# Prologue projections as three float32r products, with a narrower weight ring and subtractions on GpSimd

## What is computed

```python
def token_mixer(h, w_in, b_in, ...):
    p = h @ w_in + b_in
    y_a = hyena_branch(p[..., :ML_START], ...)
    y_b, state = mlstm_branch(p[..., ML_START:GATE_START], p[..., GATE_START:MERGE_START], ..., state0)
    g_a, g_b = jnp.split(jax.nn.sigmoid(p[..., MERGE_START:]), N_BRANCHES, axis=-1)
    y = (g_a * (y_a @ w_branch_hy) + g_b * (y_b @ w_branch_ml)) @ w_out
    return y, state

# first block, x and ctx both (1, 256, 1024)
ada_x = jnp.split(s_lat @ w_ada[l] + b_ada[l], 6, axis=-1)          # modulation, likewise ada_c
pc = hc @ w_in[l][:, ML_START:MERGE_START] + b_in[l][ML_START:MERGE_START]
_, ctx_state = mlstm_branch(pc[..., :ML_COLS], pc[..., ML_COLS:], ..., mlstm_zero_state(B))
yx, _ = token_mixer(hx, *mix_params, rows, GRID_W, ctx_state)
x = x + ada_x[2][:, None, :] * yx
x = x + ada_x[5][:, None, :] * expert_choice_ffn(hx2, w_router[l], w_exp1[l], w_exp3[l], w_exp2[l])
```

## Time and profile before

| | us |
|---|---|
| median of three runs | 2400.16 |
| lowest, highest | 2399.78, 2400.80 |
| profiled execution, its own time | 2399.33 |
| its span | 2397.5 |
| TensorE products busy | 2026.2 (85%) |
| VectorE busy | 823.2 (34%) |
| ScalarE busy | 596.3 (25%) |
| GpSimd busy | 0.2 (4 instructions) |
| DMA | 660.82 MB, 276 GB/s on average |
| mean granted TensorE clock | 0.916 of 2.4 GHz |

### The profile page before, as it was taken

The page is one execution under the profiler, slowest core; times in us unless marked ns, Lnnn a source line. Parts: engine busy times, 40 slices in busy tenths (PEclk is TensorE's granted clock), DMA queues, the critical chain, the costliest instruction groups (busy, mean ns, idle before and its releaser), DMA issues.

```text
span 2397.5 us, 28400 instructions
## 1 busy us (share of the span) xinstructions
PE 2026.2 (85%) x12394; PEld 1414.0 (59%) x12394; DVE 823.2 (34%) x1053; ACT 596.3 (25%) x698; POOL 0.2 (0%) x4
## 2 busy tenths in 40 slices
PE   7999997666666667666666899999999999989998
PEld 3586673222222222222222799888999999888998
DVE  4423523000000000000001655566555555557554
ACT  3311201000000000000001433563434433554333
POOL 0000000000000000000000000000000000000000
PEclk9999998888888877778888899999999999999999
DMA  9137255999999999999999445434544545434542
GB/s 395 71 145 329 88 236 216 436 429 432 433 430 432 433 429 434 431 429 434 431 429 430 156 180 197 185 124 152 199 176 176 224 176 195 186 120 150 197 181 97
DMA packets 34092, 660.82 MB, mean 276 GB/s; under 512 B 3784, under 2 KB 4296, under 8 KB 6224
## 3 DMA queue, kind: packets, MB, share of 16 engines
q1 hardware_dynamic: 31984, 651.60, 66.0%
q10 hardware_dynamic: 2016, 7.84, 0.9%
HBM read 658.38 MB, written 1.05 MB: 275 GB/s over the span
## 4 chain that ended last, share of the span: by engine, by line
PE 63%; DMA 29%; DVE 5%; ACT 2%; issue 1%; SPq 0%; ACTq 0%; DVEq 0%
PE ps L1329 62%; DMA ring_b<-experts_dram 19%; DMA ring<-experts_dram 9%; PE ps L1338 1%; DVE ring_lo L1104 1%; ACT w_hi L579 1%; DVE mixer_area L1254 0%; DVE att_area L1250 0%; ACT att_area L700 0%; ACT expert_area L558 0%; DVE tail L942 0%; DVE u_lo L1145 0%; DVE tail L949 0%; ACT u_hi L610 0%; DVE area_h L1084 0%
## 5 line engine op out<-in xcount | busy, mean ns | idle before, releaser
L1104 DVE TENSOR_TENSOR ring_lo<-ring,w_hi 128x2048 fp32r<-128x2048 f32 x168 | 384.9, 2292 | 242.0 <-ACT w_hi L579 242.0
L1329 PE MATMUL ps<-u_hi,w_hi 128*128 128x256 f32 x1536 | 435.5, 284 | 0.0
L1329 PE MATMUL ps<-u_hi,ring_lo 128*128 128x256 f32 x1536 | 432.8, 282 | 0.0
L1329 PE MATMUL ps<-u_lo,w_hi 128*128 128x256 f32 x1536 | 432.0, 281 | 0.0
L579 ACT CAST w_hi<-ring 128x2048 fp32r<-128x2048 f32 x168 | 320.0, 1905 | 201.5 <-PE ps L1329 200.4
L1329 PEld LDWEIGHTS ps<-u_lo,w_hi 128*128 128x128 f32 x1536 | 291.5, 190 | 1.8
L1329 PEld LDWEIGHTS ps<-u_hi,w_hi 128*128 128x128 f32 x1536 | 289.7, 189 | 2.5 <-issue 0.7
L1329 PEld LDWEIGHTS ps<-u_hi,ring_lo 128*128 128x128 f32 x1536 | 289.5, 188 | 0.0
L1329 PE MATMUL ps<-ring,area_h 128*32 128x512 f32 (+1 forms) x1088 | 185.3, 768 | 70.4 <-DMA ring<-experts_dram 62.6
L1329 PE MATMUL ps<-ring_b,area_h 128*32 128x512 f32 x1024 | 160.9, 792 | 81.0 <-DMA ring_b<-experts_dram 72.6
L558 ACT COPY expert_area<-ps 128x1024 f32<-128x1024 f32 x16 | 16.2, 1012 | 616.3 <-PE ps L1329 616.3
(11 more groups left out here) (311 smaller groups left out, 2126.6 us busy)
## 6 DMA issues: line engine op xcount, KB each, us to landing
ring<-stream_dram SPq DMA_DIRECT2D x116, 2048.0 KB, 8.0
ring_b<-experts_dram SPq DMA_DIRECT2D x48, 4096.0 KB, 31.0
ring<-experts_dram SPq DMA_DIRECT2D x48, 4096.0 KB, 31.0
area_n<-norm_rows_dram ACTq DMA_DIRECT2D x6, 512.0 KB, 4.5
tail<-filt_out_dram SPq DMA_DIRECT2D x1, 1536.0 KB, 6.5
tables<-tabs_dram ACTq DMA_DIRECT2D x1, 1408.0 KB, 13.2
tabs<-tabs_dram ACTq DMA_DIRECT2D x1, 1296.0 KB, 10.4
x_tok<-x_dram SPq DMA_DIRECT2D x1, 1024.0 KB, 9.7
```

The source lines that it names most:

```text
L1104: V.tensor_tensor(ring_lo[:, n % RING, :], ring[:, n % RING, :], upper_part(n).bitcast(F32), ALU.subtract).then_inc(sig("alone_ready") if ...
L1329: ins = M.matmul(out, lhsT, rhs, start=start, stop=stop, **more)
```

## The change

All projections of the prologue (gates, k, q, v, o, Hyena, merge, branches, output) become three float32r products. The modulation products and the short ones (filters, spectra, states, heads, transforms, router) stay float32.

The parts:

- **Inputs.** The normed, modulated input is kept as upper and lower float32r parts, `xT` for x and `cT` for the context, apart from each other. ScalarE writes the upper parts from PSUM, VectorE writes exact copies (`exact`) and subtracts. The gates' weights, the branch inputs (`y_r`) and the merged sums (`merge_r`) are split too; the merged sum of one k takes four VectorE operations instead of two.
- **Weights.** 30 of the slots are split. ScalarE casts each (`upper_first`) into one of three upper buffers: `x_r`, which lies over `x_tok`, and the former ring places 6 and 7; from the 25th on `area_hr` takes the place of `x_r`. The lower part is written over the slot, for 12 slots by VectorE (`lower_first`), for 18 (`BY_POOL`) by GpSimd, which had no work before. x is loaded a second time, since `x_r` overwrites it.
- **Ring.** After the first eight slots the ring has six places (three pairs), not eight. There are 54 slots, not 56.
- **Order.** Gates and k are computed together in passes over k; the context follows the x part. v comes ahead of q. In the loop over q and Hyena each turn is two units and two modulation slots (rows 1 and 2 both), so that the heads have no modulation. o is computed between the context states. All 16 merge units come after those. The merge units 25 to 31 are kept without the sigmoid, which then runs once over all seven. The branches are done in half passes of four k, mLSTM branch first.
- **Waits.** The second half of the first expert's blocks waits for all 54 slots.

```diff
+FIRST_RING = 6
+ADA_SLOTS = (tuple(range(8)), (13, 14, 16, 17, 19, 20, 22, 23), (25, 26, 28, 29, 31, 32, 34, 35))
+FIRST_SPLIT = (8, 9, 10, 11, 12, 15, 18, 21, 24, 27, 30, 33) + tuple(range(36, FIRST_SLOTS))
+BY_POOL = (0, 1) + tuple(range(12, 28))
+HEAD_UNITS = ((25, 26), (27,), (28, 29), (30,))
...
+            for i in range((FIRST_SLOTS - RING) // 2):
+
+                sp.wait_ge(sig("slot_used"), 2 * i + (2 if i < 3 else 4))
+                if 2 * i + 4 == FIRST_SPLIT[21] + 1:
+                    sp.dma_start(x_tok[:, :, :], d["x"]).then_inc(sig("x_loaded"), 16)
+                load(i % 3, PAIRS + i)
...
+            def upper_first(i):
+
+                n = FIRST_SPLIT[i]
+                act.wait_ge(sig(f"pair_loaded{first_place(n) // 2}"), first_turn(n) * 16 + 16)
+                if i == 0:
+                    act.wait_ge(sig("norm_ready"), TT)
+                elif i < 3:
+                    act.wait_ge(sig("slot_used"), RING)
+                else:
+                    act.wait_ge(sig("slot_used"), FIRST_SPLIT[i - 3] + 1)
+                A.copy(first_upper(i), ring[:, first_place(n), :]).then_inc(sig("first_hi"), 1)
...
+            for i in range(8):
+                upper_first(6 + i)
+                for c in (4 + 2 * i, 5 + 2 * i):
+                    to_conv(c, col("b_q", c - 4) if c < 8 else col("b_hy", c - 8), T)
...
+            def lower_first(i):
+
+                dve.wait_ge(sig("first_hi"), i + 1)
+                at = first_place(FIRST_SPLIT[i])
+                V.tensor_tensor(ring_lo[:, at, :], ring[:, at, :], first_upper(i).bitcast(F32),
+                                ALU.subtract).then_inc(sig("first_lo"), 1)
...
+                total = expert_area[:, 2048 + k % 2 * T:2048 + (k % 2 + 1) * T]
                 step(V.tensor_tensor(m, bank(k % 4), m, ALU.mult))
-                V.tensor_tensor(merge[:, k, 0, :], merge[:, k, 0, :], merge[:, k, 1, :],
-                                ALU.add).then_inc(sig("merged"), 1)
+                step(V.tensor_tensor(total, merge[:, k, 0, :], merge[:, k, 1, :], ALU.add))
+                step(V.tensor_copy(merge_r[:, k, 0, :], total))
+                V.tensor_tensor(merge_r[:, k, 1, :], total, merge_r[:, k, 0, :].bitcast(F32),
+                                ALU.subtract).then_inc(sig("merged"), 1)
...
+        @block.gpsimd
+        def _(pool):
+            for i in BY_POOL:
+
+                pool.wait_ge(sig("first_hi"), i + 1)
+                at = first_place(FIRST_SPLIT[i])
+                nc.gpsimd.tensor_tensor(ring_lo[:, at, :], ring[:, at, :], first_upper(i).bitcast(F32),
+                                        ALU.subtract).then_inc(sig("first_lo_p"), 1)
...
+            def unit(b, i, j):
+
+                w = split_first(i)
+                for k in range(KD):
+                    a = j * 1024 + k * P
+                    last = k == KD - 1
+                    product3(b[:, 0:T], [v[:, a:a + P] for v in w], [v[:, k, :] for v in xT], k == 0, last,
+                             free=int(last and j == 1), ready=sig("unit_ready") if last else None)
...
+            for i in range(8):
+                for j in range(2):
+                    unit(unit_bank(5 + 2 * i + j), 4 + i, j)
+                if i % 4 == 0:
+                    pe.wait_ge(sig("v_kept"), 1 if i == 0 else 2 * TT)
+                ada(4 if i < 4 else 7, range(2 * (i % 4), 2 * (i % 4) + 2), 1 + i // 4)
+                if i == 5:
+                    ada_turn(1, 4)
```

More of the change, by code:

```diff
@@ new lines, in _ @@
+            for k in range(KD):
+                pe.wait_ge(sig("hT_hi"), 1 + k + 1)
+                for u in range(4):
+                    for p in range(2 if u < 3 else 1):
+                        mm(bank(u)[:, 0:T], first_four(u, p, k), xT[0][:, k, :], start=k == p == 0, stop=False)
+                if 1 <= k <= 4:
+                    pe.wait_ge(sig("hT_tmp"), k)
+                    turned_in(k + 3)
+            pe.wait_ge(sig("first_lo_p"), 2)
+            for k in range(KD):
+                pe.wait_ge(sig("hT_lo"), 1 + k + 1)
+                for u in range(4):
+                    mm(bank(u)[:, 0:T], first_four(u, 0, k), xT[1][:, k, :], start=False,
+                       stop=u < 3 and k == KD - 1)
+                    if u == 3:
+                        mm(bank(u)[:, 0:T], first_four(u, 1, k), xT[0][:, k, :], start=False, stop=k == KD - 1)
@@ new lines, in with_context @@
+            def with_context(u, b):
+                for k in range(KD):
+                    if u == 0:
+                        pe.wait_ge(sig("hT_lo"), 1 + KD + k + 1)
+                    last = k == KD - 1
+                    product3(b[:, T:], [first_four(u, p, k) for p in range(2)], [v[:, k, :] for v in cT],
+                             k == 0, last, free=int(last and u % 2 == 0 and u > 0),
+                             ready=sig("unit_ready") if last else None)
+            for u in range(4):
+                with_context(u, bank(u))
@@ L1450, in _ @@
+            pe.wait_ge(sig("unit_kept"), 1)
+            for k in range(KD):
+                product3(bank(0)[:, 0:T], [first_four(4, p, k) for p in range(2)], [v[:, k, :] for v in xT],
+                         k == 0, k == KD - 1)
+            with_context(4, bank(0))
             for t in range(2 * TT):
                 for k in range(KD):
-                    w = slot(12 + k // 4)
+                    w = split_first(2 + k // 4)
                     a = (k % 4) * 512
-                    mm(bank(4 + t), hT[:, k, t * P:(t + 1) * P], w[:, a:a + 512], start=k == 0, stop=k == KD - 1,
-                       free=int(t == 3 and k % 4 == 3), ready=sig("v_ps") if k == KD - 1 else None)
@@ L1595, in branches @@
+            for first in (0, 4):
+                for g in (1, 0):
+                    pe.wait_ge(sig("hT_lo"), 1 + 2 * KD + 2 - g)
+                    for k in range(first, first + 4):
+                        w = split_first(22 + k // 2)
+                        if first and g == 1:
+                            pe.wait_ge(sig("merged"), k - 3)
                         for i in range(4):
                             a = (k % 2) * 1024 + g * 512 + i * P
-                            last = g == 1 and i == 3
```

453 lines of the change are left out of this document (242 added, 211 removed).

## The result

The changed kernel takes 2411.87 us (median of five runs, 2410.27 to 2414.56), the kernel before 2400.80 us beside it: a ratio of 1.0047, 95% interval 1.0032 to 1.0061. It is **slower by 11 us**, where the prediction had it 10 us faster. The profiled execution after took 2412.05 us (span 2410.3), that of before 2399.33.

The account below looks back on a forecast made before the run. TensorE was taken to bound the prologue, transfers the experts, so the end follows the prologue. 43.9 saved - 6.1 - 18.3 - 6.2 - 2.7 = 10.6 us off 2400.2, so 2390 us; range 2379 to 2413.

Parts of the forecast that it names:

- The bound: Prologue bound by TensorE, experts by transfers; the kernel's end moves by as much as the prologue's end.
- The products: Prologue projections on TensorE: three float32r products replace each float32 one, saving 43.9 us of 369.7.
- The start: First projection: PE waits for slot 8's cast and GpSimd's subtraction, plus transposes and clock; 6.1 us late.
- my upper bound of 3.8: High-end price in us of one GpSimd subtraction, taken as two ScalarE passes over 2048 columns; used in the forecast.
- The ring: q/Hyena loop with six ring places: three PE stops of 4.4 us, each with one clock drop; 18.3 us lost.
- The clock charge of 1.7 us each: Each PE stop at a late ring slot drops the clock to 1.2 GHz, losing 1.7 us.
- The first o unit: Slot 36, subtracted on GpSimd: PE waits 4.5 us and drops its clock once more (1.7); 6.2 us lost.
- VectorE beside GpSimd: VectorE steps waiting for GpSimd's subtractions: no term in the forecast's sum, 0 us.
- rival 2: VectorE and GpSimd exclude each other: +5.8 at last convolutions, +10 at merge sums, some +1 at a head; 2407 us; chance 0.31.
- the heads, Hyena and output: After the o units: head chains, z copy eviction, merge sums and first norm together lose 2.7 us.

Follow-up runs that it names:

- e1_vector: Changed kernel with all 18 GpSimd subtractions moved into VectorE's program, GpSimd doing nothing: 2390.3 us.
- e7_fill: e1_vector plus unread filler products on TensorE ahead of the first projection, the three late split ring slots and during the top-k search: 2383.7 us.
- e4_no_merge: Changed kernel with the subtractions of the last four slots before the output moved from GpSimd to VectorE, between its merge sums: 2403.1 us.
- e5_no_conv: Changed kernel with the subtractions of slots 36 and 37 (o units) moved from GpSimd to VectorE, at the last convolutions: 2404.3 us.

## Why the prediction was wrong, step by step

**The bound** held: with the end of the prologue at +13.6 us the time came out at +12.7. The distance from the last output product to the fifth block isn't a constant, though: 38.6 us before, 37.9 after, 42.8 in e1_vector, 35.7 in e7_fill, by how much of the router and the gather runs at 1.2 GHz. I took it as fixed.

**The products, 43.9 us**, were over-sized by 5.7. I priced 256 columns at 0.119 us a product from rows in the midst of a run. A slot of 48 products in the prologue is followed by the next work after 140.72 - 134.78 = 5.94 us, not 5.71:

```profile
134.78 6.01 PE L1457 MATMUL ps<-area_hr,ring_lo 128*128 128x256 f32 x48
140.72 1.92 PE L1457 MATMUL ps<-ring,silu_c 128*32 128x512 f32 x16
```

Inside, the starts are 0.12 us apart; 0.2 us are lost where one group of products ends and another begins. For 22 slots that is 5.1, and 0.6 for the 64 products of 512 columns, whose three parts follow each other at 0.2333 us, 0.70 for 0.69. By that the saving was 38.2 us.

**The start, 6.1 us**: under-sized by 3.4. The first product came at 51.20, not 49.8: slot 8's cast began at 44.5, and GpSimd took 4.51 us. There the page of the Trainium skill that I named beside my sum (GPSIMD Engine Reference, Elementwise — side-by-side cycle accounting: 4.5 us) was right and my upper bound of 3.8, two ScalarE passes, wrong. And the clock stood at 1.2 GHz until 57.0 us, 2.9 us lost where I had 0.9.

**The ring, 18.3 us**: over-sized by 5.0. The three stops are where I put them, each with its clock drop. What was mis-sized is the stop: 3.33 + 3.18 + 2.45 = 9.0 us, for three times 4.4. From the end of a late slot's products to the start of the next late slot it was 12.9 us (132.93 to 145.83), not 13.9: the pair landed in 7.4 us, not 8.0, and the semaphores took less than I gave them. The work in between was 9.7 us, not 9.5, and longer ahead of the third, where four transposes of the modulation rows stand too.

```profile
132.93 1.92 PE L1457 MATMUL ps<-ring,silu_c 128*32 128x512 f32 x16
```

The clock charge of 1.7 us each was nearly right: the 48 products behind the stops took 7.33, 7.41 and 7.41 us where a slot at the full clock takes 5.94, together 4.3 more. Stops and slow work are 13.3 us. Undone, the ring gives back 15.6 to 16.7 us, the o unit's share with it.

**The first o unit, 6.2 us**: right. It starts at 188.80, as the working has it.

**VectorE beside GpSimd, 0 in the forecast**: this is the step that failed. In it, GpSimd was a slower VectorE that cost latency and nothing else, and the wait of VectorE's SBUF steps for GpSimd's subtraction stood at nothing; rival 2, the exclusion, had 0.31 because no row could show it. What the runs showed in its place: steps of 0.35 and 0.48 us took 4.34 and 4.66 us beside GpSimd, and without GpSimd the whole took 21.6 us less. From the kernel without GpSimd: of the 25.5 us by which its last output product is earlier, some 5 are latency at the start and the o unit (2.1 and 2.9), and 20.5 are what exclusion costs, less what VectorE's own subtractions add (the split is read from how much earlier each stage starts, and takes in the clock behind the stops): 5.9 by the start of the heads, 3.0 in the heads, nothing in the Hyena orders, 10.3 by the start of the output, the rest behind it. Rival 2 had the places, 5.8 and 10 and 1, and 2407 to 2410 us; it was the right mechanism, missing 5 us for the products and 2 in the heads. That 2411.9 us lies within the stated range (2379 to 2413) is due to this rival, which the range took in; the forecast itself had the sign wrong.

**The sum of the misses**: 5.7 + 3.4 - 5.0 + 20.5 = 24.6 us for the 24.2 found. What is left, -0.4, is within what the heads, Hyena and output (2.7) may be off by; they weren't measured apart.

**What I can't say.** Why the clock fell at 364.8 us in one kernel and at 398.4 in another, with the same work from the last output product on, isn't settled; the two groups of times in e4_no_merge and e5_no_conv, some 5 us apart, may have the same cause. Nor do the runs say why the clock held behind one stop of 3 us and fell behind another, or why two pairs took 9 us to land in e7_fill.

## What to carry to other kernels

Before work goes to GpSimd, list the VectorE instructions that will run beside it and lie on the critical path: each one with only SBUF operands, however small, cost up to a whole GpSimd instruction in this kernel; here 41 us of VectorE time saved cost 20 us of the path, and doing the work on VectorE in its idle places was 21.6 us faster. Where a ring's round trip is the bound, draw the line at the request: work behind it hides in the round trip, work ahead of it (here the late slot's own products, slow or fast) counts in full. A shorter chain helps most; letting the needed slot land ahead of its neighbour, in 5 us for 7.4, was worth 16 us with the clock drops that it took away. Price a product from a stretch that contains the changes from one group to the next, not from the midst of one.

## What the runs showed that I had not expected

- A VectorE copy with a single SBUF input (128x256, float32 to float32r, 0.29 us) is held by GpSimd like the rest: 4.47 us. So is `TENSOR_SCALAR`: 4.34 for 0.35. An add with one PSUM operand isn't: 0.69 us.
- The two engines take strict turns. Between two GpSimd instructions in a row VectorE gets exactly one held step in, in the rows read here, also when the pieces are 1.1 us long; and GpSimd waits for VectorE too (128x1024: 4.51 us beside a VectorE subtraction of 2.29, 2.40 where VectorE was the one that waited; four pieces 5.35 us for 4.51 in one).
- Between late slots of the ring the distance is the first one's products plus 12.8 to 13.0 us, whatever the clock: 5.91 us of products gave 18.79, 8.63 gave 21.62, and the stop stayed at 3.2 to 3.3.
- A faster pace ahead of a request can be lost in the transfer: asked for 1.5 us earlier behind its late slot, a pair took 9.0 us for 7.3 and gave the same 20.4 us. One case, and its cause is open.
- Filler products change which stretch is slow also far behind them: with 15 of them ahead of it, the gather's 32 products took 5.04 us, without 7.03.
